# A two-layer hybrid decoder step on one core: first units split plane by plane, the first group evicted ahead of the parameters, another last stage

## The reference

```python
def trunk(x, states, p):
    for l in range(DEPTH):
        y, st_new = token_mixers(rmsnorm(x, p['norm_mix_g'][l]), st, p, l)
        x = x + y
        hn = rmsnorm(x, p['norm_ffn_g'][l])
        x = x + (dense_ffn(hn, p, l // 2) if l % 2 == 0 else moe_ffn(hn, p, l // 2))
    return rmsnorm(x, p['norm_final_g']), new_states
```

## Time and profile before

| | |
|---|---|
| median of three runs | 911.87 us (911.35 to 913.0) |
| the profiled execution | 909.72 us |
| its span, first to last instruction | 908.0 us |
| granted PE clock, mean | 0.993 |
| PE busy | 864.4 us, 95% |
| DVE busy | 711.5 us, 78% |
| ACT busy | 561.8 us, 62% |
| chain that ended last | PE 81%, ACT 9%, DVE 7% |

### The profile page before, as it was taken

How to read it: one execution, slowest core, us unless ns; L and a number is a source line. 1 busy time by engine, 2 the same in 40 slices (tenths; PEclk the granted TensorE clock), 3 DMA queues, 4 the chain that set the end, 5 groups by cost and what they waited for, 6 DMA issues and landing times.

```text
span 908.0 us, 14162 instructions
## 1 busy us (share of the span) xinstructions
PE 864.4 (95%) x5426; PEld 769.9 (85%) x5426; DVE 711.5 (78%) x930; ACT 561.8 (62%) x633; POOL 46.9 (5%) x98
## 2 busy tenths in 40 slices
PE   4999989999999999999999999999999999999993
PEld 4997889999999999977987788878787878888881
DVE  4798895755556446998888988888888888888888
ACT  5427985444435335258964777776878677777751
POOL 2000012200000000010102000000000000000040
PEclk9999999999999999999999999999999999999998
DMA  8831137997436556610255999999999999999981
GB/s 327 338 111 45 47 112 286 397 421 284 140 126 240 191 184 244 262 48 1 105 191 214 340 344 400 368 371 359 385 376 383 368 357 383 363 393 356 389 308 49
DMA packets 39864, 240.74 MB, mean 265 GB/s; under 512 B 5016, under 2 KB 5368, under 8 KB 19056
## 3 DMA queue, kind: packets, MB, share of 16 engines
q1 hardware_dynamic: 32432, 208.01, 60.4%
q0 software_dynamic: 5936, 27.19, 7.7%
q10 hardware_dynamic: 1440, 4.77, 1.3%
HBM read 215.01 MB, written 25.51 MB: 265 GB/s over the span
## 4 chain that ended last, share of the span: by engine, by line
PE 81%; ACT 9%; DVE 7%; issue 2%; DMA 1%; DVEq 0%; ACTq 0%
PE ps L508 11%; PE ps L509 11%; PE ps L510 11%; PE ps L818 9%; PE ps L820 9%; PE ps L819 9%; PE ps L832 4%; PE ps L834 4%; PE ps L833 4%; ACT whi L949 1%; PE ps L531 1%; PE ps L451 1%; PE ps L840 1%; DVE low L1671 1%; DVE xtok L1871 1%
## 5 line engine op out<-in xcount | busy, mean ns | idle before, releaser
L1671 DVE TENSOR_TENSOR low<-raw,whi 128x2048 fp32r<-128x2048 f32 (+1 forms) x144 | 300.2, 2109 | 47.0 <-ACT whi L1183 46.6
L1183 ACT ACTIVATE whi<-raw 128x2048 fp32r<-128x2048 f32 (+1 forms) x144 | 253.4, 1780 | 72.3 <-DMA raw<-in_w_experts 57.5
L508 PE MATMUL ps<-nhi,whi 128*128 128x264 f32 x560 | 162.1, 290 | 17.0 <-DVE low L338 13.1
L949 ACT ACTIVATE whi<-raw 128x2048 fp32r<-128x2048 f32 (+1 forms) x60 | 109.3, 1826 | 109.9 <-PE ps L510 108.7
L338 DVE TENSOR_TENSOR low<-raw,whi 128x2048 fp32r<-128x2048 f32 (+1 forms) x60 | 130.5, 2179 | 45.6 <-ACT whi L949 45.5
L509 PE MATMUL ps<-nlo,whi 128*128 128x264 f32 x560 | 160.6, 287 | 0.0
L510 PE MATMUL ps<-nhi,low 128*128 128x264 f32 x560 | 159.8, 285 | 0.0
L818 PE MATMUL ps<-whi,ehi 128*128 128x512 f32 (+1 forms) x384 | 146.4, 381 | 1.9 <-issue 1.1
L820 PE MATMUL ps<-whi,elo 128*128 128x512 f32 (+1 forms) x384 | 144.3, 376 | 0.0
L819 PE MATMUL ps<-low,ehi 128*128 128x512 f32 (+1 forms) x384 | 144.3, 376 | 0.0
L508 PEld LDWEIGHTS ps<-nhi,whi 128*128 128x128 f32 x560 | 106.7, 191 | 18.3 <-issue 17.0
(11 more groups left out here) (394 smaller groups left out, 1334.8 us busy)
## 6 DMA issues: line engine op xcount, KB each, us to landing
raw<-in_w_experts SPq DMA_DIRECT2D x104, 1024.0 KB, 7.0
raw<-in_w_dense SPq DMA_DIRECT2D x54, 1024.0 KB, 5.0
raw<-in_w_experts SPq DMA_DIRECT2D x32, 768.0 KB, 6.6
xs<-zero POOLq DMA_DIRECT2D x5, 2560.0 KB, 32.1
Cs<-in_state_c POOLq DMA_DIRECT2D x2, 2064.0 KB, 10.6
out_new_s<-Cs POOLq DMA_DIRECT2D x2, 2064.0 KB, 8.2
raw<-in_w_experts SPq DMA_DIRECT2D x8, 512.0 KB, 6.1
xe<-xs SPq DMA_DIRECT2D x7, 512.0 KB, 8.7
```

The costliest lines, as they stand in the source:

```text
L508: pe.matmul(o, hi[:, k, c], h_k, start=first, stop=False)
L949: act.activation(whi[:, u % NHI, 0:n], raw[:, u % NRAW, 0:n], ACT.Copy).then_inc(hi_done, 1)
L1183: act.activation(high_slot(odd, c)[:, 0:kt * w], raw[:, c % NRAW, 0:kt * w], ACT.Copy).then_inc(hi_done, 1)
L1671: dve.tensor_tensor(low[:, c % NRAW, part], raw[:, c % NRAW, part], high_slot(odd, c)[:, part].bitcast(F32), ALU.subtract).then_inc(lo_don ...
```

## The change

At the start SP issues all of x and the first unit in four pieces (x0, half of unit 0, its other half, x1) and unit 1 goes without a wait; the mixer weights move behind unit 5. In layer 0 ACT and DVE make normalised plane and weight plane alternately, with a semaphore for each plane, and PE has a loop of its own, `first_group`, that runs a plane's 12 matmuls when it is there and the norm's matmuls after the second plane of unit 1. Six matmuls on the identity (`warm_up`) come ahead. In both layers ACT's sigmoid and DVE's eviction of group 0 move ahead of the parameters (layer 0) or the diagonals (layer 1), and the split of the fifth unit (U+4) comes right behind. At the end the last sums are made in halves of 512 columns, ACT squares with an accumulated output in place of DVE's statistics, the root's table is loaded ahead, and the sums of the next tile stand between a tile's sums and its scaled row. Some semaphores are merged.

```diff
-            mixer_weights_before = {FIRST_UNIT[0] + 4: 0, FIRST_UNIT[20] + 6: 1}
+            mixer_weights_before = {FIRST_UNIT[0] + 6: 0, FIRST_UNIT[20] + 6: 1}
+            half0 = slice(0, UNIT // 2)
+            sp.dma_start(xT[:, 0:4, :], a["x"][:, 0:4, :]).then_inc(S["x0_in"], 16)
+            sp.dma_start(raw[:, 0, half0], a["w_dense"][0, :, half0]).then_inc(S["first_in"], 16)
+            sp.dma_start(raw[:, 0, UNIT // 2:], a["w_dense"][0, :, UNIT // 2:]).then_inc(raw_in[0], 16)
+            sp.dma_start(xT[:, 4:8, :], a["x"][:, 4:8, :]).then_inc(S["x1_in"], 16)
             for u, (_, _, _, w, ks) in enumerate(UNITS):
-                if u == 1:
-                    sp.wait_ge(S["x1_in"], 16)
+                if u == 0:
+                    continue
                 if u == 3:
                     parameters()
                 if u in mixer_weights_before:
...
+            def first_group():
+
+                for u in range(2):
+                    hi, lo = unit(whi, u, 4, PB), unit(low, u, 4, PB)
+                    for k in range(4):
+                        if k < 3:
+                            pe.wait_ge(S["first_hi"], 3 * u + k + 1)
+                            pe.wait_ge(S["first_lo"], 3 * u + k + 1)
+                        else:
+                            split_ready(u)
+                        kx = 4 * u + k
+                        for i in range(4):
+                            o, c = bank(i, T), slice(i * P, (i + 1) * P)
+                            pe.matmul(o, hi[:, k, c], nhi[:, kx, :], start=(kx == 0), stop=False)
+                            pe.matmul(o, hi[:, k, c], nlo[:, kx, :], start=False, stop=False)
+                            last = pe.matmul(o, lo[:, k, c], nhi[:, kx, :], start=False, stop=(kx == KT - 1))
+                        if (u, k) == (1, 1):
+                            norm(0)
+                    last.then_inc(used, 1)
...
+            pe.wait_ge(S["const_done"], 1)
+            warm_up(6, 7)
             pe.wait_ge(S["const_done"], 2)
             for l in range(DEPTH):
-                for g in range(2):
-                    group(20 * l + g, nhi, nlo)
+                if l == 0:
+                    first_group()
+                else:
+                    group(20, nhi, nlo)
+                group(20 * l + 1, nhi, nlo)
                 group(20 * l + 2, nhi, nlo, (0,))
                 conv_b(l)
                 group(20 * l + 2, nhi, nlo, (1,))
...
                     pe.wait_ge(S["last_y"], 2 if j else half + 1)
-                    last = pe.matmul(bank(LAST_BANKS[j] + half, PB, n), pickT[:, t0:t0 + n], ysb[:, half * PB:(half + 1) * PB], start=True, stop=True)
-                last.then_inc(S["last_ps"], 1)
+                    pe.matmul(bank(LAST_BANKS[j] + half, PB, n), pickT[:, t0:t0 + n], ysb[:, half * PB:(half + 1) * PB], start=True, stop=True).then_inc(S["last_ps"], 1)
...
-            act.dma_start(xT[:, 0:4, :], a["x"][:, 0:4, :]).then_inc(S["x0_in"], 16)
-            act.dma_start(xT[:, 4:8, :], a["x"][:, 4:8, :]).then_inc(S["x1_in"], 16)
...
                 if l == 0:
-                    act.wait_ge(S["x0_in"], 16)
                     act.wait_ge(S["gain_in"], 16)
-                norm_high(2 * l, 0)
-                hi(U)
-                if l == 0:
-                    act.wait_ge(S["x1_in"], 16)
-                    norm_high(0, 1)
-                    hi(U + 1)
+                    for u in range(2):
+                        act.wait_ge(S[f"x{u}_in"], 16)
+                        for k in range(4):
+                            n_ = act.activation(nhi[:, 4 * u + k, :], xT[:, 4 * u + k, :], ACT.Copy, scale=N_(4 * u + k, NORM_ROW[0]))
+                            if k == 3:
+                                n_.then_inc(S["norm_hi"], 1)
+                            if (u, k) == (0, 0):
+                                act.wait_ge(S["first_in"], 16)
+                            elif (u, k) in ((0, 2), (1, 0)):
+                                act.wait_ge(raw_in[u], 16)
+                            c = slice(k * PB, (k + 1) * PB)
+                            act.activation(whi[:, u, c], raw[:, u, c], ACT.Copy).then_inc(S["first_hi"] if k < 3 else hi_done, 1)
                 else:
+                    norm_high(2, 0)
+                    hi(U)
                     hi(U + 1)
                     norm_high(2, 1)
                 norm_square(2 * l)
                 hi(U + 2)
                 norm_root(2 * l)
                 hi(U + 3)
+                act.wait_ge(S["ga_in"], l + 1)
+                act.activation(sga[:, :, :], sga[:, :, :], ACT.Sigmoid).then_inc(S["sga_done"], 1)
+                hi(U + 4)
                 if l == 0:
                     parameters_out()
-                act.wait_ge(S["ga_in"], l + 1)
-                act.activation(sga[:, :, :], sga[:, :, :], ACT.Sigmoid).then_inc(S["sga_done"], 1)
                 act.wait_ge(S["mix_w"], 16 * MIX_DMAS * (l + 1))
                 wk = wg[:, :, :].rearrange("p (h j) g -> p h j g", j=3)[:, :, 1, :]
                 act.activation(wk, wk, ACT.Copy, scale=float(P) ** -0.5).then_inc(S["wk_scaled"], 1)
-                hi(U + 4)
                 hi(U + 5)
...
+            act.preload_act_table(ACT.Sqrt)
             for j, (_, n) in enumerate(TILES):
-                act.wait_ge(S["fin_ms"], j + 1)
-                act.activation(rcol[0:n, j:j + 1], ms[0:n, j:j + 1], ACT.Sqrt, bias=EPS).then_inc(S["fin_rt"], 1)
+                act.wait_ge(S["fin_sum"], j + 1)
+                step(act.activation(xe[0:n, :], xtok[0:n, j, :], ACT.Square, accum_out=ms[0:n, j:j + 1]))
+                settle()
+                act.activation(rcol[0:n, j:j + 1], ms[0:n, j:j + 1], ACT.Sqrt, scale=1.0 / D, bias=EPS).then_inc(S["fin_rt"], 1)
...
                 if l == 0:
-                    norm_low(0, 0)
-                    lo(U)
-                norm_low(2 * l, 1)
-                if l == 0:
-                    lo(U + 1)
+                    for u in range(2):
+                        for k in range(4):
+                            if k < 3:
+                                dve.wait_ge(S["first_hi"], 3 * u + k + 1)
+                            else:
+                                dve.wait_ge(hi_done, u + 1)
+                            kx = 4 * u + k
+                            n_ = dve.scalar_tensor_tensor(nlo[:, kx, :], xT[:, kx, :], N_(kx, NORM_ROW[0]), nhi[:, kx, :].bitcast(F32), ALU.mult, ALU.subtract)
+                            if k == 3:
+                                n_.then_inc(S["norm_lo"], 1)
+                            split_low(dve, u, slice(k * PB, (k + 1) * PB)).then_inc(S["first_lo"] if k < 3 else lo_done, 1)
+                else:
+                    norm_low(2, 1)
                 lo(U + 2)
                 norm_rms(2 * l)
                 lo(U + 3)
+                dve.wait_ge(used, U + 2)
+                dve.wait_ge(S["pads"], 8 * l + 3)
+                settle()
+                scaled(sga[:, :, :], 2, 2).then_inc(S["ga_in"], 1)
+                scaled(apad[:, :, 30:30 + T], 0, 2).then_inc(free[0], 1)
+                lo(U + 4)
                 if l == 0:
                     parameters_out()
-
-                dve.wait_ge(used, U + 2)
-                if l == 1:
+                else:
                     conv_b_diagonals(l)
-                dve.wait_ge(S["pads"], 8 * l + 3)
-                settle()
-                scaled(sga[:, :, :], 2, 2).then_inc(S["ga_in"], 1)
-                scaled(apad[:, :, 30:30 + T], 0, 2).then_inc(free[0], 1)
                 dve.wait_ge(S["sga_done"], l + 1)
                 dve.wait_ge(free[0], freed(20 * l))
...
                         expert(r * NE + e * 2, False)
                         expert(r * NE + e * 2 + 1, True)
             settle()
-            dve.wait_ge(S["gates_done"], 1)
             dve.wait_ge(S["fin_gain"], 16)
-            for j, (_, n) in enumerate(TILES):
+            def early_sums(j):
+
+                n = TILES[j][1]
                 dve.wait_ge(S[f"picked{j}_in"], 32)
                 for k in range(2):
                     step(dve.scalar_tensor_tensor(xtok[0:n, j, :], picked[0:n, k, j, :], early_gate[0:n, j, k:k + 1], xtok[0:n, j, :], ALU.mult, ALU.add))
                     settle()
-            for j, (_, n) in enumerate(TILES):
-                dve.wait_ge(S["last_ps"], j + 1)
-                own_rows = ps[0:n, LAST_BANKS[j]:LAST_BANKS[j] + 2, :].rearrange("p b c -> p (b c)")
-                step(dve.scalar_tensor_tensor(xtok[0:n, j, :], own_rows, last_gate[0:n, j:j + 1], xtok[0:n, j, :], ALU.mult, ALU.add))
-                settle()
+
+            def last_sums(j):
+
+                n = TILES[j][1]
                 for half in range(2):
-                    step(dve.bn_stats(bst[0:n, j, half, :], xtok[0:n, j, half * PB:(half + 1) * PB]))
-                settle()
-                token_squares(j, n)
-                settle()
```

(46 more changed lines are left out.)

8 lines of the change are left out of this document (2 added, 6 removed).

## The result

| | before | after |
|---|---|---|
| median, six executions each | 913.04 us (911.35 to 917.13) | 905.26 us (903.43 to 906.74) |
| the profiled execution | 909.72 us | 905.73 us |
| its span | 908.0 us | 903.9 us |
| granted PE clock, mean | 0.993 | 0.986 |
| PE busy | 864.4 us | 874.0 us |

The ratio is 0.9914, 95% interval 0.9892 to 0.9937: 7.8 us faster, where 10.3 were forecast. 905.26 lies 0.3 above the upper end of the range and 3.7 above the forecast of 901.6: 2.5 of that is gain that was missing (10.3 - 7.8), 1.2 is the base, whose median came out at 913.04 for the 911.87 that the forecast started from. Over all timed executions of this study the kernel before has a median of 913.0 (58) and the changed one 905.15 (18): again 7.8. The two profiled executions are only 4.0 apart, because that of before was 3.3 under its own median.

The account below looks back on a forecast made before the run. PE held 81% of the chain, so gains were sought where it waits or other engines hold the chain: end 5.8 plus start 4.5 is 10.3, taking the 911.87 median to 901.6; 8-in-10 range 899.2 to 905.0.

Parts of the forecast that it names:

- The end: Last three tiles: moving statistics from DVE to ACT and reordering rows ends the last row at 899.95 for 905.76, gain 5.8.
- Rival 3: Tile roots at the end: Square not in the root's table, loads of 1.28 before each, total gain 5.6, 906.3; chance 0.02.
- Transfers and planes: Layer 0's opening: gains at 6.0, half of unit 0 at 5.9, unit 1 at 11.1, PE starting at 8.3, not 13.12.
- the start: Layer 0's opening: earlier transfers and planes bring xbp 4.1 earlier and ktok 4.5 earlier, the gain that carries through.
- The clock in the first unit: First unit's matmuls: six warm-ups put PE at the 2.4 GHz level, 0.12 a matmul, unit 0 ending at 14.1.
- rival 1: Half of unit 0 at the lower clock, 27 matmuls at 0.22: root 2.6 later, start 1.9, 904.2; chance 0.16.
- What follows the root: Layer 0 behind the norm's root: DVE is the bound, not PE; root at 21.0, xbp at 39.9, ktok at 78.0.
- Layer 1: Same reordering in layer 1: group out at 361.9 instead of 365.1, xbp 372.3 against 372.23, so no gain.
- Rivals 2 and 4: Opening: 2, gains and x0 at 7.1 (902.6) or gains at 5.0 (900.9), 0.12 each; 4, lower clock persists, 920, 0.02.
- the reordering: Opening transfers: unit 1 lands at 11.1 instead of 13.44; if reordering did nothing, start about 2.8, 903.3, chance 0.05.
- the clock rival: Another name for rival 1: lower clock through half of unit 0, sum 7.7, 904.2; chance 0.16.

Follow-up runs that it names:

- the end alone: Kernel before with only the new last stage: median 907.32 us against 913.01, ratio 0.9939.
- the trace whose clock stayed up: Trace from the second set of executions of the unchanged changed kernel, six warm-ups: set median 902.57 us, ratio 0.9887 to the kernel before.
- the recorded trace: First profiled execution of the changed kernel, nothing altered: 905.73 us, in a set with median 905.26.
- start alone: Changed kernel with the old last stage: median 910.26 us against 913.01 for the kernel before, ratio 0.9969.
- the planes ahead: Changed kernel with thirteen warm-ups and old eviction order, a unit's activation planes made before its weight planes: 905.52 us, ratio 0.9922 to the kernel before.
- ten warm-ups: Kernel with the planes ahead and old eviction order, ten warm-up matmuls for thirteen: median 902.35 us against 913.63 for the kernel before, ratio 0.9878.
- the old order: Changed kernel with thirteen warm-ups, parameters or diagonals again ahead of first group's eviction and sigmoid: 904.36 us, ratio 0.9908 to the kernel before.
- the second trace of before: Kernel before unchanged, traced once more: 916.97 us in one execution, span 915.2.

## Why the prediction came out as it did

**The end, 5.8: right.** 5.8 in the trace, 5.7 by the median of the end alone. The steps held too: with the early sums 1.68 later, the last row's end moves from the forecast 899.95 to 901.63, and it is at 901.67. The accumulated output is an instruction of 0.19, inside the bound of 0.2. Rival 3 (table loads) is out.

**Transfers and planes: mis-sized by up to 1.5.** Gains at 4.7 to 5.2 (forecast 6.0); first half of unit 0 at 6.9 to 7.5 (5.9); unit 1 at 12.1 to 12.7 (11.1). The sum took 0.41 MB/us, from a stretch with whole units, for unit 0 in halves; the halves moved at 193 to 310 GB/s over 4 to 6. The early gains made up for nothing, since ACT then waited for weights. PE began at 8.8 to 9.4 instead of 8.3, so 0.5 to 1.1 of the start never came; in the trace whose clock stayed up it is 0.5 at the root (21.47 for 21.0).

**The clock in the first unit: the step that failed.** The forecast took the upper level with rival 1 at 0.16. The rival's mechanism is right and its price too (27 matmuls at 0.22 were worked out as 2.6; the recorded trace has some 26, and from first matmul to root 15.32 for 12.58, so 2.7; the other 0.5 of its 3.2 is the later landing; the falls in mid-unit cost 1.5 and 1.75), but it came in three traces of four with six warm-ups, not as the exception: mean lateness of the four roots (3.2 + 1.5 + 1.75 + 0) / 4 = 1.6. The reason given against it, that PE had stood still for 0.8 at the end and then ran on at full pace, didn't bear on holes of 1.9 to 3.2 us. These were longer than the forecast 1.5 because the first half landed late, and in the recorded trace also because the warm-ups ended at 6.14 for the forecast 6.8. The Trainium skill ("TensorE: Matmul & The Clock Gate", "Part 1: The HAM clock gate") says that the number of slow matmuls differs between runs of one kernel; the traces agree: 26, none, and about 15 beginning at 10.

**What follows the root.** From root to `xbp` 18.9 (forecast 39.9 - 21.0 = 18.9), from `xbp` to `ktok` 38.15 (38.1): both right. DVE is the bound there, and PE's lead is lost, as said. The new order, the group ahead of the parameters, costs 0.3 at `xbp`. The forecast's sum held that loss (root 4.4 earlier, `xbp` 4.1; DVE idle for 2.0 where it was 1.22), but did not call it a price of the order.

**Layer 1: right in size.** From Square to `xbp` 23.94 in both kernels. That the start's gain carries through is seen up to there: layer 1's Square is at 344.38 for 348.29 in the trace whose clock stayed up in the first units, still 3.9 earlier. Behind it the traces can't tell: from that Square to the first early sum it takes 533.6, 535.3 and 540.9 in the three traces with the old start and 534.7 to 539.3 in the eleven with the new one, and by the first early sum of that same trace only 0.4 of the lead is left (883.14 for 883.55).

**Sum.** At the upper level the start brings 25.38 - 21.47 = 3.9 at the root, 3.6 at `xbp`, 3.9 at `ktok` (4.5 forecast). Less 1.6 for the mean lateness of the root that is 2.3, beside 2.75 and 2.1 by medians (start alone; 7.8 less 5.7). With 5.8: 8.1, measured 7.8. Of the 2.5 that are missing, 0.6 is thus the transfers and 1.6 the lateness of the root, nearly all of it the clock. The remaining 0.3 is below what the runs can tell, and so are, by medians alone, these two shares; they rest on the landmarks. Rivals 2 and 4: the gains were early, but useless; the reordering did bring unit 1 forward, by 0.8 to 1.3, not 2.3; nothing like a loss of 14 occurred, since the lower level never lasted beyond the 6.5 us of the recorded trace.

**The range.** It left nearly 1 for the median's own scatter, taken from three executions, and 0.8 above the clock rival's 904.2. Medians of six of the changed kernel itself came out at 905.26, 902.57 and 905.93: any one of them is good to about 2, and one of the three lies inside the range. So that the first fell 0.3 outside is in part the luck of the draw, as is the base, 1.2 higher in the later set; that the centre was 2.5 too optimistic about the gain is not. What decides whether a later stretch, near 50, 80, 411 or 496, comes in an execution isn't settled. Filling the hole by other means than more warm-ups wasn't tried, nor was six warm-ups with the planes ahead.

## What to carry to other kernels

When a stage is moved forward so that TensorE waits in short holes, cost it at both clock levels and ask how long the hole is when the transfer comes late: here ten warm-ups, which end as the first plane is ready, together with the planes ahead and the old order, gave the forecast landmarks (root 21.2, `xbp` 39.85, `ktok` 78.0). Before crediting a reordering, find who waits for the result; PE's 2.5 of lead were worth nothing with DVE as the bound. And take the base from several executions: one profile of the kernel before was 3.3 under its median, another of the same code 4.0 above.

## What the hardware showed that was not expected

- The lower level comes back for some 3 us in mid-kernel, in some executions and not in others: one stretch at 428 in the first trace of before, five in the second, four in the recorded trace of the changed kernel beside that in its first unit, none in that of the end alone. All 24 in the fourteen traces begin at four places of the work, three of them the same in both layers, some 330 apart: at 47 to 52 and 383; at the keys' transposes, 77 to 83 and 406 to 414; at 95 and 424 to 428; and at 491 to 499. One in the transposes made them 2.82 for 1.53, another 2.36.
- In the opening stretch the granted clock reads 1.00 while matmuls are 0.22 apart (the first 24 in the second trace of before, 28 in the 6 us of this row, for 50 at the pitch of 0.12). There the pitch is the evidence, not the column:

```profile
13.00:19.00 6.00, 5.82 (x28) 5.85 (x29) 3.97 (x7) 5.60 (x4) 0.00 (x0) 1.00 1.02 417
```

- A unit moved in two halves ran at 193 to 310 GB/s where the same bytes in one transfer ran at 393 to 434.
- An accumulated output of ACT adds an instruction of its own, 0.19.
